# Gate/up of two token groups by seven block products instead of eight

## The reference, cut to what matters

```python
h = (layer_norm(x) * (1.0 + sc2) + sh2).astype(dt)          # (tokens, 1024)
gu = h @ w_gu[l]                                            # (tokens, 2 * 2816)
ff = ((jax.nn.silu(gu[..., :D_FF]) * gu[..., D_FF:]) @ w_down[l]).astype(jnp.float32)
x = layer_norm(DEEPNORM_ALPHA * x.astype(jnp.float32) + g2 * ff, ln2_g[l], ln2_b[l]).astype(dt)
```

## Time and profile before

| | us |
|---|---|
| median of three runs | 2813.1 (2812.8 to 2814.64) |
| the profiled execution | 2812.3 |
| its span | 2810.6 |
| TensorE busy | 2641.1 (94%) |
| DVE, ACT, POOL busy | 1647.1, 1118.5, 641.5 |
| gate/up and down, first group | 350.5 and 170.9 |
| gate/up and down, second group | 343.2 and 170.9 |
| gate/up and down to the end, third group | 257.1 and 157.9 |

### The profile page before, as it was taken

One profiled execution on the slowest core, in us unless ns is written; L12 is line 12 of the kernel. 1 busy time (PEld: TensorE's weight loads), 2 busy tenths in 40 slices (PEclk: granted clock), 3 DMA queues, 4 the chain that ended last, 5 costly groups with the idle time before them and its releaser, 6 DMA issues.

```text
span 2810.6 us, 39293 instructions
## 1 busy us (share of the span) xinstructions
PE 2641.1 (94%) x15824; PEld 1438.6 (51%) x15824; DVE 1647.1 (59%) x2121; ACT 1118.5 (40%) x1576; POOL 641.5 (23%) x865
## 2 busy tenths in 40 slices
PE   6899987789898988999999999999999999999998
PEld 3444443334343434455566665446666544899733
DVE  4657655499999999888723233544232344644454
ACT  1522211288888888323422223222222322333331
POOL 1200000166666667233311110001111000111100
PEclk8899998899999999999999999999999999999999
DMA  6225665532222211323122223542322335333453
GB/s 229 92 69 210 221 205 187 141 82 75 73 69 70 53 23 61 108 75 112 57 83 75 75 83 105 156 137 83 98 61 76 101 125 180 114 101 91 125 183 122
DMA packets 262536, 308.16 MB, mean 110 GB/s; under 512 B 27693, under 2 KB 221037, under 8 KB 256602
## 3 DMA queue, kind: packets, MB, share of 16 engines
q1 hardware_dynamic: 262362, 305.76, 35.3%
HBM read 267.32 MB, written 38.40 MB: 109 GB/s over the span
## 4 chain that ended last, share of the span: by engine, by line
PE 69%; DVE 15%; issue 5%; ACT 3%; DMA 2%; POOL 1%; SPq 0%; POOLq 0%; DVEq 0%; ACTq 0%
PE ps L2004 33%; PE ps L2038 17%; PE ps L1716 7%; DVE work L1366 3%; PE ps L1955 3%; DVE work L1382 3%; PE ps L1806 2%; PE ps L1830 2%; PE ps L1808 1%; ACT ps L947 1%; DVE work L1363 1%; DVE work L1530 1%; DVE wmax L1116 1%; PE ps L1845 1%; DMA work<-in_w_down 1%
## 5 line engine op out<-in xcount | busy, mean ns | idle before, releaser
L2004 PE MATMUL ps<-hidden_t,work 128*128 128x384 f16 (+2 forms) x7392 | 944.5, 289 | 0.6 <-DVE work L1580 0.6
L2004 PEld LDWEIGHTS ps<-hidden_t,work 128*128 128x128 f16 x7392 | 646.3, 97 | 297.5 <-issue 0.7
L2038 PE MATMUL ps<-work 128*128 128x512 f16 (+1 forms) x2244 | 489.3, 379 | 0.0
L1716 PE MATMUL ps<-hidden_t,work 128*128 128x512 f16 (+1 forms) x1920 | 366.9, 350 | 11.8 <-DVE hidden_t L1139 7.3
L2038 PEld LDWEIGHTS ps<-work 128*128 128x128 f16 (+1 forms) x2244 | 215.7, 98 | 272.7 <-issue 17.8
L726 POOL TENSOR_TENSOR work<-work 128x512 f32<-128x512 f32 (+2 forms) x320 | 304.9, 955 | 201.6 <-DVE work L1366 128.6
L1577 DVE SCALAR_TENSOR_TENSOR work<-ps,col,work 128x384 f32<-128x384 f32 (+1 forms) x154 | 80.9, 525 | 432.5 <-ACT work L1044 432.4
L783 POOL TENSOR_TENSOR work<-work 128x384 f16<-128x384 f32 (+1 forms) x154 | 118.1, 767 | 932.7 <-ACT work L1046 932.7
L1586 DVE SCALAR_TENSOR_TENSOR work<-work,col 128x1024 f16<-128x1024 f32 x132 | 167.8, 1280 | 226.4 <-ACT work L1050 226.4
L1716 PEld LDWEIGHTS ps<-hidden_t,work 128*128 128x128 f16 x1920 | 166.0, 100 | 201.9 <-issue 28.4
L1050 ACT ACTIVATE work<-work,col 128x1024 f16<-128x1024 f32 x132 | 150.3, 1147 | 289.5 <-PE ps L2038 275.4
(11 more groups left out here) (206 smaller groups left out, 2447.0 us busy)
## 6 DMA issues: line engine op xcount, KB each, us to landing
work<-in_w_gu SPq DMA_DIRECT2D x132, 512.0 KB, 5.1
work<-in_w_down SPq DMA_DIRECT2D x132, 512.0 KB, 3.7
work<-in_w_ada SPq DMA_DIRECT2D x24, 1024.0 KB, 5.4
work<-in_w_gu SPq DMA_DIRECT2D x22, 1024.0 KB, 6.0
work<-in_w_down SPq DMA_DIRECT2D x11, 1024.0 KB, 6.3
work<-in_x_prompt SPq DMA_DIRECT2D x8, 1024.0 KB, 7.1
work<-in_w_in SPq DMA_DIRECT2D x16, 512.0 KB, 6.4
out<-work SPq DMA_DIRECT2D x32, 256.0 KB, 2.5
```

The costliest lines, as they stand in the source:

```text
L1716: mm = pe.matmul(bank(blk, n, blk), B_HL[s][:, wh * KD * P + k * P:wh * KD * P + (k + 1) * P], moving(k, xh, blk), start=(k == 0 and (wh, ...
L2004: mm = pe.matmul(out, E_GHL[s][:, wh, k, w, :], x, start=(k == 0 and (wh, xh) == (0, 0)), stop=(k == KD - 1 and (wh, xh) == TERMS[-1]))
L2038: mm = pe.matmul(ps[0:rows, 2 * slot + half, :], E_HID[:, j, xh, at:at + rows], E_DHL[slab_home(g)][:, wh, 512 * half:512 * (half + 1)], s ...
```

## The change

In groups 2 and 3 the chunk becomes a 2 x 2 block product. The weights are cut into gate and up and into k blocks 0 to 3 and 4 to 7, the tokens into two halves of 384 (272 in the third group: two tiles and half of the sample tokens) and the same two halves of k. Seven products of 4 k by 3 terms replace eight: 84 matmuls a chunk, of 384 or 272 columns. Their operands are sums and differences of blocks in f32, which are then split into high and low parts.

- Token operands: four, formed once a group on POOL (`operands`, `gather_last`), during the down passes of the group before, over the tiles of `hidden_t` no longer needed.
- Weight operands: seven sets a chunk, `E_SET`, in a ring of ten; four of them come from sums that POOL forms in `E_SUM` (`weight_sums`, three buffers), three straight from `E_GRAW`. ACT writes each high part (`set_high`), DVE each low part (`set_low`), 512 elements each.
- Results: `products` puts product 0 to 3 in four banks and adds 4, 5 and 6 to the first three after ACT has copied them out (`copy_out`); DVE adds them up (`form`) and gates (`gated`, `product`). A chunk uses four banks, the next the other four.
- `E_GRAW` stays one buffer, and `E_DRAW` and `E_SUM` now lie over it and behind it: the next chunk is loaded after `set_low` number 6, and a group's first chunk after the last slab's low part. The slabs have five homes.
- Statistics and norms of the three older tiles stand in chunks 0 to 5. The first group keeps its eight products; the scales have a factor 4 of room for the sums; the gate rows are partly made later; three semaphores of the start are merged.

The core of the diff:

```diff
-            def next_gu(c):
-                sp.wait_ge(gu_lo, c)
-                load_gu(c % NF)
+            def next_gu(grp, j):
+                if grp == 0:
+                    sp.wait_ge(gu_lo, j)
+                elif j == 0:
+                    sp.wait_ge(wd_lo, 2 * NF * grp)
+                else:
+                    sp.wait_ge(gu_lo, split_n(grp, j - 1, 6))
+                load_gu(j)
...
+            def weight_sums(grp, j, which):
...
+                    if i == 0:
+                        pool.wait_ge(gu_raw, 32 * (NF * grp + j + 1))
+                    if 4 * n + i >= 3:
+                        last = 4 * n + i - 3
+                        pool.wait_ge(gu_lo, split_n(1, last // 4, (1, 2, 4, 5)[last % 4]))
+                    if i >= 2:
+                        pool.wait_ge(summed_w, 4 * n + (1, 3)[i - 2])
+                    a, b, op = ((u_lo, u_hi, ALU.add), (g_lo, u_lo, ALU.subtract),
+                                (out[0], g_lo, ALU.subtract), (g_hi, out[2], ALU.subtract))[i]
+                    pool.tensor_tensor(out[i], a, b, op).then_inc(summed_w, 1)
...
+            def set_high(grp, j, i):
...
+                act.activation(E_SET[set_home(grp, j, i)][:, 0, :, :], src, ACT.Identity,
+                               scale=c1(C_SGU)).then_inc(gu_hi, 1)
...
+            def chunk(grp, j):
+                more = j + 1 < NF
+                if j:
+                    hid_high(grp, j - 1, 0)
+                    hid_high(grp, j - 1, 1)
+                copy_out(grp, j, A1)
+                if more:
+                    set_high(grp, j + 1, 0)
+                else:
+                    dn_split(2 * NF * grp)
+                copy_out(grp, j, T5)
+                if more:
+                    for i in (1, 2, 3):
+                        set_high(grp, j + 1, i)
+                else:
+                    dn_split(2 * NF * grp + 1)
+                sigmoid(grp, j, 0)
+                if more:
+                    set_high(grp, j + 1, 4)
+                copy_out(grp, j, U2)
+                if more:
+                    set_high(grp, j + 1, 5)
+                    set_high(grp, j + 1, 6)
+                sigmoid(grp, j, 1)
...
+            def set_low(grp, j, i):
...
+                v.wait_ge(gu_hi, split_n(grp, j, i))
+                v.scalar_tensor_tensor(home[:, 1, :, :], src, c1(C_SGU), home[:, 0, :, :],
+                                       ALU.mult, ALU.subtract).then_inc(gu_lo, 1)
...
+            def chunk(grp, j):
+                more = j + 1 < NF
+                if j:
+                    finish(grp, j - 1)
+                if more:
+                    set_low(grp, j + 1, 0)
+                else:
+                    dn_low(2 * NF * grp)
+                if j < 6:
+                    (counted, normed)[j % 2](6 * grp - 3 + j // 2)
+                if more:
+                    set_low(grp, j + 1, 1)
+                form(grp, j, T57).then_inc(formed, 1)
+                if more:
+                    set_low(grp, j + 1, 2)
+                    set_low(grp, j + 1, 3)
+                else:
+                    dn_low(2 * NF * grp + 1)
+                form(grp, j, C11).then_inc(formed, 1)
+                if more:
+                    set_low(grp, j + 1, 4)
+                v.wait_ge(formed, formed_n(grp, j, C11))
+                gated(grp, j, 0).then_inc(formed, 1)
+                v.wait_ge(copied, copied_n(grp, j, U2))
+                own.done(v.tensor_tensor(E_T5[:, 0:WIDTH[grp]], E_T5[:, 0:WIDTH[grp]], E_U2[:, 0:WIDTH[grp]], ALU.add))
+                if more:
+                    set_low(grp, j + 1, 5)
+                    set_low(grp, j + 1, 6)
+                form(grp, j, C12).then_inc(formed, 1)
+                v.wait_ge(formed, formed_n(grp, j, C12))
+                step(gated(grp, j, 1))
...
+            def products(grp, j):
+                bank0 = 4 * ((j + grp + 1) % 2)
+                for i in range(7):
+                    bank = bank0 + (0, 1, 2, 3, 0, 1, 2)[i]
+                    pe.wait_ge(gu_hi, split_n(grp, j, i))
+                    pe.wait_ge(gu_lo, split_n(grp, j, i))
...
+                    elif i == 4:
+                        pe.wait_ge(copied, copied_n(grp, j, A1))
+                    elif i == 5:
+                        pe.wait_ge(copied, copied_n(grp, j, T5))
+                    else:
+                        pe.wait_ge(formed, formed_n(grp, j, T57))
...
+                    for k in range(4):
+                        for wh, xh in TERMS:
```

More of the change, by code:

```diff
@@ L662, in _ @@
                         x1_in(second[(15, 17, 19).index(j)][0])
-                    if j == 11 and grp < 2:
-                        next_gu(NF * (grp + 1))
             for n in (14, 15, 16):
@@ L788, in rstd_e @@
                 rstd(E_STAT[n % 3]).then_inc(e_rstd, 1)
+            def weight_sums(grp, j, which):
+                n = NF * (grp - 1) + j
+                gate, up = E_GRAW[:, :, 0, :], E_GRAW[:, :, 1, :]
+                g_lo, g_hi, u_lo, u_hi = gate[:, 0:4], gate[:, 4:8], up[:, 0:4], up[:, 4:8]
+                out = [E_SUM[(4 * n + i) % 3] for i in range(4)]
+                for i in which:
+                    if i == 0:
[8 more added lines that the diff above has]
+                    pool.tensor_tensor(out[i], a, b, op).then_inc(summed_w, 1)
@@ new lines, in bank_of, with copy_out @@
+            def bank_of(grp, j, which):
+                return 4 * ((j + grp + 1) % 2) + which
+            def copy_out(grp, j, what):
+                n = WIDTH[grp]
+                dst, bank, product = ((E_A1, 0, 0), (E_T5, 1, 1), (E_U2, 0, 4))[what]
+                act.wait_ge(gu_mm, product_n(grp, j, product))
+                if what == A1 and j == 0:
+                    act.wait_ge(e_res, 6 * grp)
+                elif what == A1:
+                    act.wait_ge(hid_set, hid_n(grp, j - 1, 0))
+                elif what == T5 and j:
+                    act.wait_ge(hid_lo, hid_n(grp, j - 1, 1))
+                elif what == U2 and j:
+                    act.wait_ge(formed, formed_n(grp, j - 1, C21))
+                act.activation(dst[:, 0:n], ps[:, bank_of(grp, j, bank), 0:n], ACT.Identity).then_inc(copied, 1)
@@ new lines, in sigmoid, with hid_high @@
+            def sigmoid(grp, j, blk):
+                n = WIDTH[grp]
+                act.wait_ge(formed, formed_n(grp, j, (C11, C12)[blk]))
+                if blk == 0 and j:
+                    act.wait_ge(hid_set, hid_n(grp, j - 1, 1))
+                src = (E_A1, E_C12)[blk]
+                act.activation(E_SG[:, 0:n], src[:, 0:n], ACT.Sigmoid, scale=c1(C_F1)).then_inc(sig_set, 1)
+            def hid_high(grp, j, blk):
+                n = WIDTH[grp]
+                src = (E_C21, E_T5)[blk]
+                act.wait_ge(hid_set, hid_n(grp, j, blk))
+                act.activation(E_HID[grp][:, j, 0, n * blk:n * (blk + 1)], src[:, 0:n], ACT.Identity).then_inc(hid_hi, 1)
@@ new lines, in in_bank, with form @@
+            def in_bank(grp, j, which):
+                return ps[:, 4 * ((j + grp + 1) % 2) + which, 0:WIDTH[grp]]
+            def form(grp, j, what):
+                n = WIDTH[grp]
+                dst, src, bank, product, copy = ((E_T5, E_T5, 2, 2, T5), (E_A1, E_A1, 3, 3, A1), None,
+                                                 (E_C12, E_U2, 1, 5, U2), (E_C21, E_U2, 2, 6, U2))[what]
+                v.wait_ge(gu_mm, product_n(grp, j, product))
+                v.wait_ge(copied, copied_n(grp, j, copy))
+                if what == C21 and j:
+                    v.wait_ge(hid_lo, hid_n(grp, j - 1, 0))
+                return v.tensor_tensor(dst[:, 0:n], src[:, 0:n], in_bank(grp, j, bank), ALU.add)
@@ L1641, in _ @@
                     dn_low(g0 + NF + j)
-                    if j == 2:
+                    if j == 3:
                         for n in first:
                             summed(n)
-                    if 3 <= j < 3 + 2 * len(first):
-                        (counted, normed)[(j - 3) % 2](first[(j - 3) // 2])
-                if grp < 2:
-                    gu_low(NF * (grp + 1), 0)
-                    for n, slot in PASSES[2 * grp + 1]:
-                        summed(n)
+                    if 4 <= j < 4 + 2 * len(first):
+                        (counted, normed)[j % 2](first[(j - 4) // 2])
+            for j in range(NF):
+                if j == NF - 1:
+                    for g in range(3):
+                        dn_low(g)
+                elif j:
+                    gu_low(j + 1, (j + 1) % 2)
+                hidden(j, 0)
+                hidden(j, 1)
+                if j == 0:
+                    for s in range(3):
+                        own.done(v.memset(E_STAT[s], 1.0))
+                    own.wait()
+            pass_pair(0, 3)
+            for grp in (1, 2):
+                for i in range(6):
+                    set_low(grp, 0, i)
+                for n, slot in PASSES[2 * grp - 1]:
+                    summed(n)
+                set_low(grp, 0, 6)
```

(5 more changed lines are left out.)

451 lines of the change are left out of this document (303 added, 148 removed).

## The result

The changed kernel takes 2988.26 us (2985.66 to 2990.03, four runs) against 2812.95 us (2812.57 to 2814.64, four runs): ratio 1.0623, 95% interval 1.061 to 1.0637. The forecast was 2962 us with a range of 2880 to 3015: slower, as said, and 26 us more than said.

The account below looks back on a forecast made before the run. TensorE bounds gate/up now; the single-buffer weight supply would take over, with turns of 16.9 and 16.55 us. Group 2 +36.6 and group 3 +113.4 us make 2812.3 + 150 = 2962 us, range 2880 to 3015.

Parts of the forecast that it names:

- The load: Weight load into the single raw buffer, from issue to first split: taken as 5.8 us of each chunk's turn.
- TensorE's own part: Matmul time of a chunk with 84 matmuls: 13.65 us in group 2, 9.7 in group 3.
- The step from landing to the seventh low part: Splits, sums and unmixing after a load lands: 11.1 us in group 2, 10.75 in group 3.
- the forecast's steps: Group 2 path after landing, instruction by instruction: first low part 1.7 us, T57 3.8, C11 6.8, seventh low part 11.1.
- The lock for the whole instruction: DVE and POOL excluding each other for whole instructions, no hidden handover time: sum 48 us higher than forecast.
- their tiles' norms: Older tiles' statistics and norms on DVE, chunks 0 to 5: norm about 2.3 us a tile, statistics 0.3; 8 a group.
- What stands before and behind those turns: Ends of a gate/up stage: 12 and 11.8 us before the 20 turns, 21.8 and 19.6 after the last landing.
- Nothing, as counted: Forming token operands on POOL, 80 to 90 us with gathering before group 3, covered by 171 us of down passes.
- Rival (a): Splits barely collide, no holds by POOL: turns 14.9 and 14.3 us, total 2877 us; chance 0.12.
- Rival (b): Weight supply stays hidden, TensorE stays the bound at turns of 13.65 and 9.7 us: total 2735 us; chance 0.05.
- Rival (c): Full lengths at every DVE/POOL handover, landing at 6.1 us: turns of 18.4 us, total 3022 us; chance 0.05.
- Rival (d): TensorE's granted clock drops through idle gaps, group 3 turns up to 19.4 us: 57 us more, 3019; chance 0.05.

Follow-up runs that it names:

- e8: Changed kernel with splits and sums from the second chunk on working on 32 elements instead of 512 (work left out, only to measure): 2755.16 us, ratio 0.9796.
- e3: Changed kernel with each weight sum on POOL replaced by two fills of its buffer that read nothing (sums left out): 2886.0 us, ratio 1.0265.
- e4: Changed kernel with a second raw weight buffer in group 3 and no weight sums, all seven sets split straight from the raw buffer: 2834.3 us, ratio 1.0081.
- e6: Changed kernel with a chunk's seven high and seven low parts each in one piece, unmixing no longer between them: 2937.67 us, ratio 1.044.
- e9: e6 without POOL's weight sums (left out, only to measure): 2807.09 us, ratio 0.9982.
- e11: e6 with the four weight sums formed on DVE instead of POOL, nothing left out: 2906.6 us, ratio 1.0335.
- e7: e6 plus a second raw weight buffer in group 3: 2931.38 us, ratio 1.0418.
- e12: Group 2 as in e11; group 3 with eight products over two gathered blocks of 272 columns, one split as before the change: 2823.29 us, ratio 1.0036.

## Why the prediction was right, and where its size was off

**The bound moved as said.** The load of the next chunk goes out 0.03 us after the seventh low part, the first split starts 5.4 to 6.0 us after that, and TensorE's matmuls leave the loop. TensorE's own part was well worked out too: e8 runs at 13.65 in group 2.

**The mis-sized term: the sums.** The step from landing to the seventh low part was counted at 11.1 us and is 11.72 in each of the steady chunks of group 2. The load went the other way, a mean of 5.59 from issue to first split in both groups instead of 5.8, and hides a third of it: 16.9 + 0.6 - 0.2 is the 17.34 measured. Against the forecast's steps, in the turn shown above: first low part 1.85 (1.7 counted), second 3.5 (3.2), T57 4.0 (3.8), fourth 6.9 (6.2), C11 7.35 (6.8), sigmoid 8.0 (7.4), fifth high part 8.6 (8.0), fifth low part 9.4 (8.8). The whole difference has come about by the fourth low part, and the later steps keep their counted lengths. POOL's four sums take 6.29, counted 1.1 + 3 x 1.5 = 5.6. The row at 2080.75 ends at 2081.85, 0.53 after the first sum (whose follower on ACT starts at 2081.34), close to the 0.56 counted for a low part that was waiting. The second sum ends just before 2083.02, 1.15 after that low part: counted 0.94. The hold hides part of DVE's instruction but nothing of POOL's. The first sum, 1.28 instead of 1.1, is the rest. In group 3 the same sums make 11.28 from 10.75. The lock for the whole instruction, which the prediction takes from the Trainium skill and puts 48 us above its sum, would have given 3010; the measured 2988 lies between, and a waiting low part needs 0.53 us after the sum and not its full 0.75.

**Where the 26 us are.** I compare the profiled executions, 2989.3 against 2962.3, so 27 us. From the issue of the load of chunk 1 to that of chunk 21, 20 turns, it took 357.6 and 348.6 us; with their tiles' norms 346 and 339 were counted. That is 21 us: 40 turns at 0.4 more (17.34 for 16.9, 16.90 for 16.55) are 16, and most of the rest lies in the chunks with a tile's statistics (18.0 in group 2, 0.7 more than a turn, counted 0.3) or a norm (19.9, 2.6 more, counted 2.3). What stands before and behind those turns came to 35.3 and 32.2, counted 33.8 and 31.4: 2 us. Chunk 1 is there a little sooner than counted (11.5 us after the start in both groups, counted 12 and 11.8), and the last products end later, 24.0 and 20.8 us after the last landing, counted 21.8 and 19.6. The later start is 2.5, the down pass and the end 1.1. That is all of it.

**Nothing, as counted.** Forming the operands: POOL works 87 us in the down pass of group 2, some 76 of them on gathering and forming (80 to 90 counted) and the rest on chunk 0's sums, low parts and `rstd`, beside 171.85 us of matmuls, and group 3 starts without a wait. The price that it does have is for DVE's down splits: L1884 has a mean of 1423 ns over all its 132 on the page after, 1280 in the earlier trace rows; the down pass covers it.

**Rival (a), 2877 us.** It has no holds. e3 takes precisely these away and measures 15.1 and 14.7 where (a) has 14.9 and 14.3, 2886 us in all. Its turn is thus well sized, and it fell because the sums do read SBUF.

**Rival (b), 2735 us.** e8 comes to 2755. It decides at the turn, as said, and e4 shows that a second buffer would not have been enough for it.

**Rival (c).** Full lengths at every handover would be 18.4; 17.34 is less than a third of the way there from 16.9.

**Rival (d).** The granted clock did fall, to a mean of 0.87 in group 3 and 0.96 in group 2 (windows above), with waits of TensorE in each chunk, like the 1.97 us before 2096.41 (3.32 before the same product in group 3, at 2638.52). TensorE was busy for 263 us in group 3, where 22 x 9.7 = 213 were counted at full clock, yet that cost no time that can be seen: the turn is made up of the load, DVE, ACT and POOL, without a matmul in it; no run changes the clock by itself. The Trainium skill ("TensorE: Matmul & The Clock Gate", Why this matters for your kernels, the table that the prediction calls the Summary table) warns of such gaps; here the warning holds for the clock and not for the time.

## What to carry to other kernels

Fewer matmuls pay only down to the pace of whatever feeds TensorE; before one takes matmuls away, the whole turn of a single buffer (load, high part, low part, next load) is to be added up, with all that stands in the same queues between landing and release. Extra weight blocks are paid for on the splitting engines each time they are formed, and work moved to POOL is not free for DVE if POOL reads SBUF while DVE reads two tensors there. When a limit is removed, look at which row ends the wait next: here the load gave way to a chain of short instructions over the queues of three engines that was 9 us long in group 2 of three different kernels (e6, e9, e11); the expectations for e7 and e11, and with e11's that for e12, missed for leaving it out.

## What the runs showed of the hardware that was not expected

- The mutual hold is uneven (changed kernel, the turn at 2080.00). A low part that was waiting ends 0.53 us after POOL's sum where it takes 0.75 by itself; a sum that was waiting ends 1.15 after the low part where it takes 1.09. Side by side, with the four sums on POOL, the seven low parts take 7.77 us on DVE (e6), all eleven instructions one after another on DVE alone 7.2 (e11): two engines were slower than one.
- The same sum takes 1.09 us on POOL and 0.63 on DVE (three in 1.89, e11).
- TensorE's granted clock fell to 0.87 in a stage without making that stage longer.
